# RMS norms behind the turns: raw rows turned, row factors applied to the products, first units ordered by token block

## What is computed

```python
def rmsnorm(x, g):
    xf = x.astype(jnp.float32)
    y = xf * lax.rsqrt(jnp.mean(xf * xf, axis=-1, keepdims=True) + EPS)
    return (y * g.astype(jnp.float32)).astype(x.dtype)

for i in range(DEPTH):                       # DEPTH = 2
    hn = rmsnorm(h, mix_norm[i])
    if i == 0: h = h + conformer_conv(hn, ...)        # 2048 columns, gated, causal conv of 31 taps, norm, product
    else:
        k, v, c_bhs = shared_kv(h, kv_norm, w_kvf, b_f)   # rmsnorm(h, kv_norm) @ w_kvf
        h = h + fox_attention(hn, w_q, w_o, k, v, c_bhs)
    hn = rmsnorm(h, ffn_norm[i])
    h = h + jnp.square(jax.nn.relu(hn @ ffn_w1[i])) @ ffn_w2[i]      # width 4096
    gate = jax.nn.sigmoid(rmsnorm(h, ple_norm[i]) @ ple_w_gate[i])
    h = h + gate * (p[i] @ ple_w_proj[i])
return rmsnorm(h, final_norm)
```

## Time and profile before

| what | value |
|---|---|
| median of three timed runs | 2592.39 us |
| profiled execution, its own time | 2589.41 us |
| its span in the trace | 2587.3 us |
| mean granted clock of TensorE | 0.968 |
| TensorE matmul busy | 2405.0 us (93%) |
| VectorE busy | 1806.5 us (70%) |
| ScalarE busy | 1463.2 us (57%) |
| mean read bandwidth | 227 GB/s |

### The profile page before, as it was taken

One profiled execution on the slowest core, in us unless ns is written; L12 is line 12 of the kernel. 1 busy time (PEld: TensorE's weight loads), 2 busy tenths in 40 slices (PEclk: granted clock), 3 DMA queues, 4 the chain that ended last, 5 costly groups with the idle time before them and its releaser, 6 DMA issues.

```text
span 2587.3 us, 29857 instructions
## 1 busy us (share of the span) xinstructions
PE 2405.0 (93%) x11253; PEld 1981.4 (77%) x11253; DVE 1806.5 (70%) x1720; ACT 1463.2 (57%) x1550; POOL 53.3 (2%) x97
## 2 busy tenths in 40 slices
PE   7888999877999999999999999996979998999997
PEld 6676887756888888888888888875768876777885
DVE  5675545774889898889888898986845455544454
ACT  4622434353677777777767676764754345445444
POOL 0000000002100000000000000000000000000000
PEclk9999999998999999999999999997989998999998
DMA  7203555405999999999999999976214553403541
GB/s 293 98 4 114 180 195 192 166 1 188 362 334 379 337 375 343 368 347 368 347 368 349 357 358 343 373 258 211 82 37 163 192 182 127 151 21 130 195 179 49
DMA packets 264085, 589.67 MB, mean 228 GB/s; under 512 B 8402, under 2 KB 39346, under 8 KB 263729
## 3 DMA queue, kind: packets, MB, share of 16 engines
q1 hardware_dynamic: 261376, 579.38, 61.9%
q0 software_dynamic: 2608, 8.93, 1.1%
HBM read 587.22 MB, written 1.05 MB: 227 GB/s over the span
## 4 chain that ended last, share of the span: by engine, by line
PE 80%; DVE 9%; ACT 5%; DMA 4%; issue 2%; SPq 0%; DVEq 0%; ACTq 0%
PE up L1875 15%; PE up L1877 15%; PE up L1876 15%; PE acc L1875 8%; PE acc L1876 7%; PE acc L1877 7%; DMA raw<-in_ffn_w 3%; DVE wl L1259 3%; ACT wh L767 3%; PE up L2278 2%; PE acc L2158 1%; PE up L2064 1%; PE tp L1866 1%; PE tp L2194 1%; PE acc L2050 1%
## 5 line engine op out<-in xcount | busy, mean ns | idle before, releaser
L1573 DVE TENSOR_TENSOR wl<-raw,wh 128x2048 fp32r<-128x2048 f32 x378 | 864.7, 2291 | 128.4 <-ACT wh L973 126.1
L973 ACT ACTIVATE wh<-raw 128x2048 fp32r<-128x2048 f32 x378 | 727.1, 1924 | 225.2 <-PE up L1877 135.9
L1875 PE MATMUL up<-wh,xTh 128*128 128x512 f32 x1888 | 756.5, 401 | 27.6 <-DVE wl L1259 7.7
L1877 PE MATMUL up<-wh,xTl 128*128 128x512 f32 x1888 | 742.5, 393 | 0.0
L1876 PE MATMUL up<-wl,xTh 128*128 128x512 f32 x1888 | 741.7, 393 | 0.0
L1259 DVE TENSOR_TENSOR wl<-raw,wh 128x2048 fp32r<-128x2048 f32 x171 | 389.2, 2291 | 387.7 <-ACT wh L767 386.9
L767 ACT ACTIVATE wh<-raw 128x2048 fp32r<-128x2048 f32 x171 | 324.4, 1916 | 389.6 <-PE up L1877 218.0
L1875 PEld LDWEIGHTS up<-wh,xTh 128*128 128x128 f32 x1888 | 359.6, 190 | 107.5 <-issue 20.2
L1877 PEld LDWEIGHTS up<-wh,xTl 128*128 128x128 f32 x1888 | 358.3, 190 | 77.5
L1876 PEld LDWEIGHTS up<-wl,xTh 128*128 128x128 f32 x1888 | 359.5, 190 | 71.0
L1875 PE MATMUL acc<-wh,hTh 128*128 128x512 f32 x864 | 339.7, 393 | 7.8 <-DVE wl L1573 4.8
(11 more groups left out here) (341 smaller groups left out, 1961.0 us busy)
## 6 DMA issues: line engine op xcount, KB each, us to landing
raw<-in_moe_w_gate SPq DMA_DIRECT2D x126, 1024.0 KB, 6.8
raw<-in_moe_w_up SPq DMA_DIRECT2D x126, 1024.0 KB, 7.1
raw<-in_moe_w_down SPq DMA_DIRECT2D x126, 1024.0 KB, 6.1
raw<-in_ffn_w SPq DMA_DIRECT2D x32, 2048.0 KB, 8.8
raw<-in_hg_w_in SPq DMA_DIRECT2D x7, 2048.0 KB, 13.2
raw<-in_da_w_in SPq DMA_DIRECT2D x6, 2048.0 KB, 8.2
raw<-in_ffn_w_gate SPq DMA_DIRECT2D x11, 1024.0 KB, 6.6
raw<-in_ffn_w_up SPq DMA_DIRECT2D x11, 1024.0 KB, 10.9
```

The costliest lines, as they stand in the source:

```text
L973: f(wh[:, x % SPLITS, :], raw[:, x % RAW, :], ACT.Copy).then_inc(moe["hi"], 1)
L1573: V.tensor_tensor(wl[:, x % SPLITS, :], raw[:, x % RAW, :], wh[:, x % SPLITS, :].bitcast(F32), ALU.subtract).then_inc(moe["lo"], 1)
L1875: mm(out, x_hi, w_hi, start=start, stop=False)
L1877: return mm(out, x_lo, w_hi, start=False, stop=stop)
```

## The change

RMS norms: the raw rows `h` are turned as soon as half a row (512 columns) is there (`s_h` counts those), the gain still goes in when the turned rows are read, and the row's factor `row_scale[b]` is made beside the products and applied where a product is read (scale of the activation, or an operand of the VectorE pass). Layer norms: block 0 is turned ahead of block 1's norm. The first units behind the layer norms that feed the FFN, the attention and the convolution go by token block (`unit_by_block`); the residual moves from behind unit 0 to the turns. The per-layer inputs are turned before the last down product, into their own `pe_parts`. The raw rows for keys and values are turned by column half, the first half inside the gate's last unit. The last expert's down halves are split ahead of the turned hidden rows where a buffer is free, the convolution's first two halves ahead of `expert_out`, and its first three chunks are loaded when their slots are split, not all experts' halves. Some small tiles share storage.

```diff
+BLOCKS = [(b, q) for b in range(NB) for q in range(2)]
+BLOCK = [range(2 * b, 2 * b + 2) for b in range(NB)]
+COLUMNS = [(b, q) for q in range(2) for b in range(NB)]
...
-        sp.wait_ge(moe["lo"], counter(n_extra, NE)(PASS, RAW))
-
         for i in range(4):
+            if i < RING:
+                sp.wait_ge(moe["lo"], counter(n_extra, NE)(PASS, RAW - 5 + 2 * i))
...
+        def layer_norms(turned=None, between=None, gain=None):
             for b in range(NB):
                 norm_root(sc[:, b, 1:2], sc[:, b, 0:1])
...
+                if b == 0 and between is not None:
+                    between()
+                if turned is not None:
+                    to_channels(turned, gain, places=BLOCK[b])
+
+        def mean_squares(stage):
+            for b in range(NB):
+                act.wait_ge(s_h, 2 * NB * (stage + 1) if stage in (H_Q, H_FIN) else 2 * NB * stage + 2 * b + 2)
+                n = NB * stage + b
+                if n > 0:
+                    act.wait_ge(s_sq, n)
+                f(squares, h[:, b, :], ACT.Square, accum_out=sc[:, b, 2:3]).then_inc(s_sq, 1)
+
+        def row_roots(stage):
+            for b in range(NB):
+                act.wait_ge(s_ms, NB * stage + b + 1)
+                f(sc[:, b, 1:2], sc[:, b, 0:1], ACT.Sqrt).then_inc(s_rt, 1)
+
+        def rows_from_sums(a0):
+            for b in range(NB):
+                act.wait_ge(s_acc, a0 + b + 1)
+                for q in range(2):
+                    f(h[:, b, q * W:(q + 1) * W], acc[:, 2 * b + q, :], ACT.Copy).then_inc(s_h, 1)
...
+                down = 4 if t_ < EU or following is not None else 0
+                if not down:
+                    split_half(at, t_, 0)
+                    split_half(at, t_, 1)
                 turned_hidden(at, t_)
-                down = 4 if t_ < EU or following is not None else 0
-                split_half(at, t_, down)
-                if t_ < EU or following is not None:
+                if down:
+                    split_half(at, t_, 4)
                     gate_act(at, t_)
-                split_half(at, t_, down + 1)
+                if down:
+                    split_half(at, t_, 5)
...
         last_split = len(pl.halves)
...
+        final = counter(n_extra, LAST)
+        act.wait_ge(moe["down"], final(EU, EU - 1))
+        split(1)
+        act.wait_ge(moe["used"], final(3 * EU, 3 * EU))
+        split(1)
+        expert_out(final)
 
         act.wait_ge(s_vecs, 2)
-        to_channels(T_cv, 0)
-        split(2)
+        layer_norms(T_cv, gain=0)
+        mean_squares(H_CV)
+        split(1)
+        row_roots(H_CV)
...
+                rows_from_sums(A_O1)
 
             to_channels(d["T_f"], 3 + i)
...
+            split(1)
+            mean_squares(H_F[i])
+            split(1)
+            row_roots(H_F[i])
+            act.wait_ge(s_r, NB * (H_F[i] + 1))
+            mlp(d["g_ff"], d["t_ff"], ACT.Relu, W, 2, row_scale,
+                lambda: turn_hi(d["T_p"], pe_hi, tp[:, d["T_p"] % 2, :]))
+
+            rows_from_sums(A_F1 if i else A_F0)
+            to_channels(d["T_g"], 5 + i, places=BLOCK[0])
+            split(1)
+            to_channels(d["T_g"], 5 + i, places=BLOCK[1])
+            split(1)
+            mean_squares(H_G[i])
+            row_roots(H_G[i])
             split()
+            act.wait_ge(s_r, NB * (H_G[i] + 1))
             for c in range(2):
                 split()
                 for b in range(NB):
-                    step_act(d["g_p"] + NB * c + b, half[:, b, :], up[:, b, :], ACT.Sigmoid)
+                    step_act(d["g_p"] + NB * c + b, half[:, b, :], up[:, b, :], ACT.Sigmoid, scale=row_scale[b])
+                    if i == 0 and c == 1 and b == 0:
+                        to_channels(after[1]["T_q"], 2, COLUMNS, range(2))
                 if c == 0:
                     split()
-        rms(False)
+        mean_squares(H_FIN)
+        row_roots(H_FIN)
...
+                V.tensor_scalar(sc[:, b, 0:1], sc[:, b, 2:3], 1.0 / D, RMS_EPS, ALU.mult, ALU.add).then_inc(s_ms, 1)
+
+        def row_scales(stage):
+            for b in range(NB):
+                dve.wait_ge(s_rt, NB * stage + b + 1)
+                V.reciprocal(row_scale[b], sc[:, b, 1:2]).then_inc(s_r, 1)
+            dve.wait_ge(s_r, NB * (stage + 1))
...
+                begin_root(b, stats(b, src[:, b, :]), 1.0, LN_EPS)
+                if b == 1 and turned is not None and between is None:
+                    to_channels(turned, gain, places=BLOCK[0])
...
+        last_split = len(pl.halves)
+        split(2)
         expert_out(final)
-        for n in range(4):
+        for n in range(2):
             add(final, n, give_banks[n])
...
+        dve.wait_ge(s_vecs, 2)
+
+        def add_second():
+            for n in range(2, 4):
+                add(final, n, give_banks[n])
+            dve.wait_ge(moe["added"], final(4, 8))
+
+        dve.wait_ge(moe["added"], final(4, 6))
+        layer_norm(y, turned=T_cv, between=add_second, gain=0, halves=True)
+        mean_squares(H_CV)
+        split(1)
+        row_scales(H_CV)
...
+        def unit_by_block(g0, t0, enter):
+
+            halves = [next_half(4) for _ in range(2)]
             for b in range(NB):
-                g = g0 + NB * c + b
-                if c == 0 and t0 is not None:
-                    xT_ready(b, t0)
+                g = g0 + b
+                enter(b, 0)
                 if g >= 2:
                     pe.wait_ge(s_st, g - 1)
...
+                for part, (q, w) in enumerate(halves):
+                    if part == 1:
+                        enter(b, 1)
+                    pe.wait_ge(s_lo, q + 1)
+                    xT_part(t0, BLOCKS, b, part)
+                    ins = half_products(up[:, g % 2, :], b, w, part)
+                    if part == 1:
+                        ins.then_inc(s_up, 1)
+                    elif b == NB - 1:
+                        ins.then_inc(s_used, 1)
...
+        def enter_ff(b, part):
+
+            if part == 0:
+                turn_block(T_ff, h, b, normed(N_LN0))
+                residual(aident, [b])
+
+        mlp(g_ff, t_ff, T_ff, 2, 1, enter_ff)
+
+        def enter_da(b, part):
+
+            if b == 0:
+                turn_block(T_da, h, part, normed(N_LN1))
+
+        project(g_da, t_da, 6, T_da, 4, enter_da)
...
+        def turn_ready(t0, stage, places, order=BLOCKS):
+
+            for x in places:
+                rows_ready(stage)(x)
+                turn_place(t0, h, x, order)
+
+        def enter_cv(b, part):
+
+            if part == 0:
+                turn_ready(T_cv, H_CV, BLOCK[b])
+
+        project(g_cv, t_cv, 4, T_cv, 2, enter_cv)
...
+                def turn_rest(part):
+
+                    if part == 0:
+                        turn_ready(d["T_q"], H_Q, range(2, 4), COLUMNS)
+
+                project(d["g_kv"], d["t_kv"], 4, d["T_q"], 4, order=COLUMNS, middle=lambda c: turn_rest if c == 0 else None)
...
+                turn_ready(d["T_f"], H_F[i], BLOCK[b])
+                residual(ident, [b])
+
+            def turn_inputs():
+
+                pe.wait_ge(s_pe, 16 * (i + 1))
+                turn_bank(d["T_p"])
+                for k in range(2):
+                    for b in range(NB):
+                        ins = nc.tensor.transpose(tp[:, d["T_p"] % 2, (2 * k + b) * P:(2 * k + b + 1) * P],
+                                                  pe_tm[:, b, k * P:(k + 1) * P], ident)
+                ins.then_inc(s_T, 1)
+
+            mlp(d["g_ff"], d["t_ff"], d["T_f"], 4, 2, before_last=turn_inputs)
...
+                turn_ready(d["T_g"], H_G[i], BLOCK[c])
+                if c == 0:
+                    pe.wait_ge(s_lo, q + 1)
+                    pe.wait_ge(s_Te, d["T_p"] + 1)
                 for b in range(NB):
...
+                    s = NB * c + b
+                    for k in range(2):
+                        ins = split_product(acc[:, s, :], pe_Th[:, k, b * P:(b + 1) * P], pe_Tl[:, k, b * P:(b + 1) * P],
+                                            w[0][:, k, c * W:(c + 1) * W], w[1][:, k, c * W:(c + 1) * W], k == 0, k == 1)
             ins.then_inc(s_used, 1)
-            project(d["g_p"], [None] * 4, 2, d["T_g"], 4)
+
+            def turn_first(part):
+
+                if part == 1:
+                    turn_ready(after[1]["T_q"], H_Q, range(2), COLUMNS)
+
+            project(d["g_p"], [None] * 4, 2, d["T_g"], 4, middle=lambda c: turn_first if i == 0 and c == 1 else None)
```

More of the change, by code:

```diff
@@ L881, in _, with mlp @@
         split(2)
-        layer_norms()
-        def mlp(g0, ts, gate, width, down_halves):
+        layer_norms(T_ff, split)
+        def mlp(g0, ts, gate, width, down_halves, scale=None, after_turns=None):
             for u in range(len(ts) // NB):
@@ L897, in mlp @@
                     turn_hi(tt, hTh[:, b, 0:width], tp[:, tt % 2, 0:width])
+                if last and after_turns is not None:
+                    after_turns()
                 if last:
                     split()
[L901 to L902 removed]
```

(60 more changed lines are left out.)

348 lines of the change are left out of this document (140 added, 208 removed).

## The result

The changed kernel takes 2561.8 us (median of 4 runs, 2560.05 to 2563.09), the kernel before 2592.35 in the same comparison: a ratio of 0.9877, 95% interval 0.9865 to 0.9890. That is 30.5 us less. The forecast was 2565.0 with a range of 2551 to 2580. The profiled execution took 2560.05 us (span 2558.2), 29.4 less than that of before.

What follows compares the result with a forecast made beforehand. TensorE, busy 93% of the span, bounds the kernel, so only its waits at layer boundaries can be won. Boundary gains of 38.2 us less 10.8 of slow clock give 27.4 net: 2565.0 us, range 2551 to 2580.

Steps and rivals of the forecast that it cites:

- B: Layer norm into the attention projection: second unit starts 1.2 us earlier, idle 4.1; -0.6 us kept after the clock.
- G: Gate 1 into keys and values: second unit starts 5.7 us earlier, idle 4.7; 3.9 us kept after the clock.
- E: Convolution into FFN 1: second unit starts 6.2 us earlier, idle 2.6; 5.3 us kept after the clock.
- H: Attention output into FFN 2: second unit starts 2.0 us earlier, idle 2.3; 1.1 us kept after the clock.
- F and I: FFN 1 and 2 into the gate: second unit 6.2 us earlier each, idle 2.4; 5.3 us kept each.
- D: End of the experts into the convolution: second unit 9.8 us earlier, idle 5.9; 8.0 us kept after the clock.
- J: Final norm: block zero's square waits for all four additions, so 1.15 us lost.
- (a): Short waits leave the clock alone and long ones are shorter: nothing paid, 38.2 us won, 2554.2 us; chance 0.17.
- (b): Splits set the pace: one more 2.3 us split on the path at five boundaries, 2576.5 us; chance 0.15.
- (d): The change does nothing: every boundary wins little and pays it in clock, 2592 us; chance 0.04.
- (c): FFN weights set the pace: chunks wait for slots, taking the gains of both FFN entries, 2571.4 us; chance 0.06.
- (e): Slower: the clock never recovers in the broken first units at nine boundaries, 2640.6 us; chance 0.03.

Runs made afterwards that it cites:

- the first four kernels with parts put back: Changed kernel with put back: gated FFN entry, 2565.69 us; attention projection entry, 2560.86; last down product's split order, 2568.39; all three plus convolution's first unit by halves, 2564.92.
- the fifth: Changed kernel with the convolution's first unit and the attention projection's first unit put back to halves behind both blocks' turns: 2557.51 us.
- the kernel with A put back: Changed kernel with the entry from the layer norm into the gated FFN put back to both norms, both turns, unit by halves: 2565.69 us.

## Why the prediction was right, step by step

**The mechanism and the sum.** The scaled rows' waits went and the second units' waits came, in the number and at the places that were forecast. Their lengths were right at B and G and too long elsewhere: 4.6, 4.1, 5.9 and 4.7 us for the long four, measured 3.69, 4.02, 3.50 and 4.56; 2.3 to 2.6 for the short ones, measured 1.96 and 1.95 at E and H, and 1.16 at the gates. The starts add up to 42 us where 38.2 were forecast, the clock took 9.5 where 10.8 were. That the total came within 2 us (29.1 against 27.4) is partly luck: single terms kept 7.9 us more than forecast and others 6.2 less.

**F and I: VectorE's splits were priced too late.** The multiply at the gate, in the changed kernel:

```profile
2134.39 4.50 DVE L1278 TENSOR_TENSOR wl<-raw,wh 128x2048 fp32r<-128x2048 f32 x2 [1.72 <-ACT wh L757]
...
2138.80 0.68 DVE L1854 TENSOR_TENSOR stage<-half,acc 128x512 f32<-128x512 f32 x1
...
2140.41 0.47 PE L1903 MATMUL up<-wh,xTh 128*128 128x512 f32 x1 [1.16 <-DVEq L1857]
```

The last matmul of the down products started at 2120.09 here, so both splits are done 18.8 us behind it; the forecast had 19.7 on the same count. With a wait of 1.16 in place of 2.4 us there was no clock to pay either, so each gate kept 2.2 or 2.3 us more than forecast.

**D: one term was missing, one had the wrong sign.** That the early splits bring the down product forward was right (1743.39 in a trace that was 0.5 us late there, forecast 1742.8) and is the larger part of D: undoing it costs 6.6 us. Missing was the load of the root table, 1.28 us between the statistics and the first norm's root, which used to lie under `expert_out`; loaded early, the first turns start 1.3 us sooner, but the second unit only 0.4. Wrong was the sign of the block order, which the forecast counted as 24 products hidden: it costs 3.4, of which 1.8 at the second unit's start. Together the two account for the 2.2 us by which that unit started later than forecast, on a common origin. The wait ahead of it was 3.50 us and not 5.9, since the first unit ended late too.

**B: the sign was right, the size too small.** 1.6 us won, 2.8 paid; the forecast had 1.2 and 1.8. The price lay within the bounds of 1.6 to 2.5 only for the other long waits: 1.6 at A and at D, 2.3 at G. The four cost 8.3 us where 7.2 were forecast.

**E, G, H** came within 0.5 us at the start. Some of that is luck too: the forecast put the old second units at 1956.6, 2193.9 and 2362.4 (2193.9 is the start of a reading in the earlier trace rows), and the trace of before has them at 1956.12, 2193.66 and 2362.13. **The short waits** were given half a price each, 3.6 us in all. In fact E and the two gates paid nothing and H 1.2, a third of that.

**J** was 0.7 us too dear: with both mean squares done together, both roots and both output passes run one behind the other without the gap that used to lie between the blocks; the changed kernel needs 0.1 us more to read the last product and 0.7 more from the last addition to the last pass, and a shorter output transfer gives 0.3 back.

**The reading with a factor** cost nearly what was taken, 0.69, and not the upper bound of 1.28: ScalarE's takes 0.69 (0.60 without), VectorE's 0.75 at L1778 and at L1728 (0.69 before). The Trainium skill (ScalarE: Activation LUTs, What ACT_TABLE_LOAD costs) gives 93 ns for an operand that is a pointer to one value for each partition; 0.60 to 0.69 agrees.

**The rivals.** (a) was half right: three of the four short waits left the clock alone and two long ones were shorter, but 9.5 us of clock were paid. (b) did not happen: every second unit but D's started at least as early as forecast, and D's 2.2 us have the two causes above. (d) held at B alone. (c) showed as 1.0 us over the whole of FFN 1, not the 6.4 that it would have taken. (e) did not happen: no unit ran slow to its end. One reading of the rows was wrong: the group of the earlier trace rows has three waits, not ten; the other boundaries' waits stand in other groups. What no step had were the 2.4 us lost between boundaries; where a slow stretch there is longer than in the trace of before, the instructions are the same, and I did not settle why.

## What to carry to other kernels

When a chain of waits is removed, ask what is handed on at the end of the first unit, and put the reader of its products ahead of any preparation that is needed later than the reader's result: that order was worth 23 us here, where the change itself brought 30. A finer order of the same products is no gain in itself: it brought 1.2 us at A and cost 2.1 at B and 3.4 at D. Where it adds waits, count each with the slow matmuls behind it. An engine that is off the bound can still be on the path for a microsecond at a time (a table load, a square that waits for the other block), and such places are found in the timeline of the boundary, never in the page's shares.

## What the runs showed of the hardware

**The length of a short wait does not fix its price.** In the changed kernel TensorE waits 1.96 us at E, and the 3.4 us behind it have a clock of 1.00; it waits 1.95 us at H, and the clock is 0.60. In the traces of the first four kernels with parts put back, of the fifth and of the one with early tables, H is slow each time; E is at full clock each time but one. That one is the kernel with only the RMS part; its second unit behind 1.96 us of waiting:

```profile
1949.80:1953.20 3.40, 3.40 (x10) 2.71 (x10) 2.93 (x3) 0.73 (x2) 0.00 (x0) 0.53 0.00 0
```

Waits of 1.1 to 1.2 us in front of a product unit were never followed by slow matmuls in these traces, nor was the one of 1.59 us at D with the readings first. The wait of 2.05 us inside the convolution's first unit was, in all seven traces that have it. Waits of 3.3 to 4.6 us in front of a second unit always were, by 5 to 13 slow matmuls; 4.02 us at B left 13 in one trace and 6 in another.

**The same code can run at either clock in two executions.** In the first layer, which all kernels share, the changed kernel's trace has a clock of 1.00; the kernel with A put back, after the same waits of 5.50 and 1.8 us, has 0.50 over 8 us. First the changed kernel, then that one:

```profile
135.00:139.00 4.00, 3.24 (x22) 2.76 (x23) 3.59 (x4) 0.74 (x1) 0.00 (x0) 1.00 0.15 18
```

```profile
135.00:143.00 8.00, 6.15 (x25) 5.38 (x24) 5.46 (x6) 1.46 (x2) 1.63 (x3) 0.50 0.21 30
```

Such stretches put some traces over 3 us behind others before the first norm. It is the reason why medians of four or five runs could not settle the small steps, and the traces' own stretches could.
